# The last expert's y summed on chip through a 0/1 matrix of slots by tokens

## What is computed

```python
def grouped_moe(x, w_router, b_router, w_gate, w_up, w_down):
    gates = shared_group_router(xt, w_router, b_router)    # two experts per token
    out = jnp.zeros_like(xt)
    for e in range(N_EXPERTS):                              # 16
        h = jax.nn.silu(xt @ w_gate[e]) * (xt @ w_up[e])
        out = out + gates[:, e:e + 1] * (h @ w_down[e])
...
x = layer_norm(DN_ALPHA * x + moe, ln2_g[l], ln2_b[l])
```

## Time and profile before

| what | value |
|---|---|
| median of 3 runs | 868.54 us |
| profiled execution, its own time | 869.28 us |
| its span in the trace | 867.6 us |
| TensorE busy | 839.5 us, 97% of the span |
| VectorE, ScalarE, GpSimd busy | 566.9, 453.4, 72.4 us |
| mean granted TensorE clock | 0.98 |

### The profile page before, as it was taken

The page is one execution under the profiler, slowest core; times in us unless marked ns, Lnnn a source line. Parts: engine busy times, 40 slices in busy tenths (PEclk is TensorE's granted clock), DMA queues, the critical chain, the costliest instruction groups (busy, mean ns, idle before and its releaser), DMA issues.

```text
span 867.6 us, 11074 instructions
## 1 busy us (share of the span) xinstructions
PE 839.5 (97%) x3810; PEld 688.0 (79%) x3810; DVE 566.9 (65%) x621; ACT 453.4 (52%) x455; POOL 72.4 (8%) x61
## 2 busy tenths in 40 slices
PE   9999999999999999999999998899999999999993
PEld 8788788888888888888888887688888888888751
DVE  4887444444449874423455846699888888889607
ACT  4555434434666653323334142497878777878610
POOL 1000000000000000000000005221122111220100
PEclk9999999999999999999999978999999999999997
DMA  7242324323233333335327653899999999999552
GB/s 202 83 115 80 97 81 138 97 78 116 79 94 102 92 113 96 96 96 178 107 85 276 260 194 98 280 365 389 372 369 366 375 371 378 365 376 370 190 222 97
DMA packets 147346, 172.14 MB, mean 198 GB/s; under 512 B 7554, under 2 KB 90123, under 8 KB 147318
## 3 DMA queue, kind: packets, MB, share of 16 engines
q1 hardware_dynamic: 142214, 161.88, 55.0%
q0 software_dynamic: 5104, 9.90, 3.2%
HBM read 163.99 MB, written 15.24 MB: 207 GB/s over the span
## 4 chain that ended last, share of the span: by engine, by line
PE 63%; DMA 18%; DVE 12%; ACT 4%; issue 2%; SPq 0%; DVEq 0%; ACTq 0%; POOL 0%; POOLq 0%
DMA est<-in_w_exp_gate_dram 18%; PE psA L613 7%; PE psA L614 7%; PE psA L615 7%; DVE elo L1356 6%; PE psB L614 5%; PE psB L615 5%; PE psB L613 5%; ACT ehi L1037 3%; PE psD L613 2%; PE psD L614 2%; PE psD L615 2%; PE psC L614 1%; PE psC L615 1%; PE psC L613 1%
## 5 line engine op out<-in xcount | busy, mean ns | idle before, releaser
L1356 DVE TENSOR_TENSOR elo<-est,ehi 128x2048 fp32r<-128x2048 f32 x96 | 218.5, 2289 | 49.2 <-ACT ehi L1037 49.0
L1037 ACT ACTIVATE ehi<-est 128x2048 fp32r<-128x2048 f32 x96 | 183.1, 1917 | 72.2 <-DMA est<-in_w_exp_gate_dram 25.0
L1157 DVE TENSOR_TENSOR wlo<-wst,whi 128x1024 fp32r<-128x1024 f32 (+1 forms) x76 | 95.0, 1250 | 91.5 <-ACT whi L877 90.4
L877 ACT ACTIVATE whi<-wst 128x1024 fp32r<-128x1024 f32 (+1 forms) x76 | 81.8, 1077 | 71.6 <-PE psB L615 30.6
L784 PE MATMUL psA<-ehi,xe_hi 128*128 128x512 f32 x256 | 101.8, 398 | 2.8 <-DVE xe_lo L1553 2.8
L785 PE MATMUL psA<-elo,xe_hi 128*128 128x512 f32 x256 | 100.3, 392 | 0.0
L786 PE MATMUL psA<-ehi,xe_lo 128*128 128x512 f32 x256 | 100.2, 392 | 0.0
L613 PE MATMUL psB<-xT_hi,whi 128*128 128x512 f32 x208 | 80.9, 389 | 0.0
L614 PE MATMUL psB<-xT_lo,whi 128*128 128x512 f32 x208 | 80.9, 389 | 0.0
L615 PE MATMUL psB<-xT_hi,wlo 128*128 128x512 f32 x208 | 80.9, 389 | 0.0
L784 PEld LDWEIGHTS psA<-ehi,xe_hi 128*128 128x128 f32 x256 | 48.4, 189 | 14.4 <-DVE xe_lo L1553 2.9
(11 more groups left out here) (287 smaller groups left out, 1520.8 us busy)
## 6 DMA issues: line engine op xcount, KB each, us to landing
est<-in_w_exp_gate_dram SPq DMA_DIRECT2D x32, 1024.0 KB, 13.7
est<-in_w_exp_down_dram SPq DMA_DIRECT2D x32, 1024.0 KB, 13.9
est<-in_w_exp_up_dram SPq DMA_DIRECT2D x32, 1024.0 KB, 12.9
wst<-in_w_in_dram SPq DMA_DIRECT2D x60, 512.0 KB, 3.9
wst<-in_w_branch_r_dram SPq DMA_DIRECT2D x8, 640.0 KB, 4.4
wst<-in_w_branch_a_dram SPq DMA_DIRECT2D x8, 512.0 KB, 3.6
o_st<-in_w_out_dram SPq DMA_DIRECT2D x8, 512.0 KB, 4.6
x1d<-x SPq DMA_DIRECT2D x8, 512.0 KB, 3.9
```

The costliest lines, as they stand in the source:

```text
L877: A(whi[p][:, 0:K, :], wst[p][:, 0:K, :], ACT.Copy).then_inc(w_hi, 1)
L1037: A(ehi[s][:], est[s][:], ACT.Copy).then_inc(gu_hi if s < 4 else d_hi, 1)
L1157: V.tensor_tensor(wlo[p][:, 0:K, :], wst[p][:, 0:K, :], whi[p][:, 0:K, :], ALU.subtract).then_inc(w_lo, 1)
L1356: V.tensor_tensor(elo[s][:], est[s][:], ehi[s][:], ALU.subtract).then_inc(gu_lo if s < 4 else d_lo, 1)
```

## The change

The y of expert 15 stays on chip. ScalarE and VectorE split it, scaled, into last_hi and last_lo; VectorE builds last_by, a matrix with a 1 where a slot's token is the column's token; TensorE adds last_by times last_hi and last_lo to each tile's sum. Expert 15's scatter is dropped, so its rows of `ys` are never written; `ys` is cleared in memory by eight stores at the place where the table is cleared. SyncE's wait before it loads `ys` is now for the scatters up to expert 14 and for gate and up of expert 15. The down product of expert 14 stands between the two halves of gate and up of expert 15. x1 is added to yg by GpSimd, tile by tile, and the x1 products and the filler are dropped.

```diff
--- before.py
+++ after.py
@@ -196,6 +196,9 @@
         hT_hi = at("hT_hi", 154, [P, KF, P], F32R)
         hT_lo = at("hT_lo", 156, [P, KF, P], F32R)
         yb = [at("yb0", 158, [P, D]), at("yb1", 72, [P, D])]
+        last_hi = at("last_hi", 72, [P, D], F32R)
+        last_lo = at("last_lo", 92, [P, D], F32R)
+        last_by = at("last_by", 104, [P, S], F32R)
         ln2_gb = at("ln2_gb", 162, [P, 2, D])
         chosen_by = at("chosen_by", 151, [P, 3, TT, P], BF16)
 
@@ -308,6 +311,10 @@
         y_evac = sem("y_evac")
         y_stored = [sem(f"y_stored{p}") for p in range(2)]
         more_stored = sem("more_stored")
+        ys_zeroed = sem("ys_zeroed")
+        last_l = sem("last_l")
+        last_listed = sem("last_listed")
+        pre_done = sem("pre_done")
         sum_done = sem("sum_done")
         ln2_landed = sem("ln2_landed")
         got = [sem(f"got{t}") for t in range(TT)]
@@ -461,7 +468,8 @@
                 sp.dma_start(ln2_gb[:, n, :], v.to_broadcast([P, D])).then_inc(ln2_landed, 16)
 
             for p in range(2):
-                sp.wait_ge(y_stored[p], (NE // 2 - p) * 16)
+                sp.wait_ge(y_stored[p], (NE // 2 - 1) * 16)
+            sp.wait_ge(gu_used, 4 * NE)
             sp.wait_ge(more_stored, more * 16 + 16)
             for t in range(TT):
                 for n in range(2):
@@ -505,8 +513,11 @@
             pool.wait_ge(tile_done, 20)
             pool.dma_start(tab.rearrange("(b p) w -> b p w", p=P), vacant[0:BLOCKS]).then_inc(tab_cleared, 16)
             pool.dma_start(x1d[ROWS:ROWS + P, :], zero[:]).then_inc(trash_zeroed, 16)
+            for n in range(2 * TT):
+                pool.dma_start(ys[n * P:(n + 1) * P, :], zero[:]).then_inc(ys_zeroed, 16)
             pool.wait_ge(tab_cleared, 16)
             pool.wait_ge(trash_zeroed, 16)
+            pool.wait_ge(ys_zeroed, 16 * 2 * TT)
 
             def gather(b, idx):
                 pool.indirect_dma_start(out=xe[b % 2][:], out_offset=None, in_=x1d,
@@ -518,7 +529,7 @@
                 pool.wait_ge(y_evac, b * 2 + 2)
                 pool.indirect_dma_start(out=ys, out_offset=bass.IndirectOffsetOnAxis(ap=idx, axis=0),
                                         in_=yb[b % 2][:], in_offset=None, bounds_check=ROWS - 1,
-                                        oob_is_err=False).then_inc(y_stored[b % 2] if b < NE - 1 else more_stored, 16)
+                                        oob_is_err=False).then_inc(y_stored[b % 2] if b < NE - 2 else more_stored, 16)
 
             pool.wait_ge(x1_stored, 32 * TT)
             pool.wait_ge(pick_done, 1)
@@ -542,7 +553,7 @@
                 gather(b, lists[:, b, 0:1].bitcast(U32))
                 if b >= 4:
                     scatter(b - 4, lists[:, b - 4, 0:1].bitcast(U32))
-            for b in range(NE - 4, NE):
+            for b in range(NE - 4, NE - 1):
                 scatter(b, lists[:, b, 0:1].bitcast(U32))
             pool.wait_ge(plan_done, 2)
             more = pool.value_load(plan[0:1, 7:8], min_val=0, max_val=BLOCKS - NE)
@@ -561,6 +572,9 @@
                     pool.indirect_dma_start(out=ys, out_offset=bass.IndirectOffsetOnAxis(ap=cur[:, 0:1].bitcast(U32),
                                                                                          axis=0),
                                             in_=yb[0][:], in_offset=None).then_inc(more_stored, 16)
+            for t in range(TT):
+                pool.wait_ge(got[t], 32)
+                nc.gpsimd.tensor_tensor(yg[:, 0, t, :], yg[:, 0, t, :], x1[:, t, :], ALU.add).then_inc(pre_done, 1)
 
 
         @block.tensor
@@ -773,9 +787,9 @@
                                       xe[p][:, k * P:(k + 1) * P], ident[:])
                 mm.then_inc(xe_t, 1)
 
-            def gate_up(b, first=False):
+            def gate_up(b, first=False, parts=range(4)):
                 pe.wait_ge(xe_l, b + 1)
-                for s in range(4):
+                for s in parts:
                     if s % 2 == 0 and not first:
                         pe.wait_ge((silu_done, h_done)[s // 2], b)
                     pe.wait_ge(gu_lo, b * 4 + (s + 1))
@@ -836,13 +850,15 @@
                 turn(2 * i, 1, xe_landed[1], i * 16 + 16)
                 turn(2 * i + 1, 0, xe_landed[0], i * 16 + 32)
             turn(NE - 2, 1, xe_landed[1], NE // 2 * 16)
-            gate_up(NE - 1)
+            gate_up(NE - 1, parts=range(2))
             down(NE - 2)
+            gate_up(NE - 1, parts=range(2, 4))
             hidden_t(NE - 1)
             down(NE - 1)
             pe.wait_ge(plan_done, 2)
             more = pe.value_load(plan[0:1, 7:8], min_val=0, max_val=BLOCKS - NE)
             with pe.If(more > 0):
+                pe.wait_ge(last_l, 2)
                 with pe.Fori(0, more) as i:
                     rows_t(i + NE, 0, more_landed, i * 16 + 16)
                     gate_up(i + NE)
@@ -850,17 +866,21 @@
                     down(i + NE)
 
             for t in range(TT):
+                pe.wait_ge(pre_done, t + 1)
                 if t == TT - 1:
                     pe.wait_ge(y_evac, (more + NE) * 2)
-                    warm(18, psB[0])
+                    pe.wait_ge(last_l, 2)
                 for h in range(2):
-                    pe.matmul(pairs[t][:, h, :], ident[:], x1[:, t, h * S:(h + 1) * S], start=True, stop=False)
-            for t in range(TT):
-                pe.wait_ge(got[t], 32)
-                for n in range(2):
-                    for h in range(2):
-                        mm = pe.matmul(pairs[t][:, h, :], ident[:], yg[:, n, t, h * S:(h + 1) * S],
-                                       start=False, stop=(n == 1))
+                    for n in range(2):
+                        pe.matmul(pairs[t][:, h, :], ident[:], yg[:, n, t, h * S:(h + 1) * S],
+                                  start=(n == 0), stop=False)
+                if t == 0:
+                    pe.wait_ge(last_listed, 1)
+                    pe.wait_ge(last_l, 2)
+                for h in range(2):
+                    for part in (last_hi, last_lo):
+                        mm = pe.matmul(pairs[t][:, h, :], last_by[:, t * P:(t + 1) * P], part[:, h * S:(h + 1) * S],
+                                       start=False, stop=(part is last_lo))
                 mm.then_inc(sum_done, 1)
 
 
@@ -963,6 +983,7 @@
 
             act.wait_ge(tab_cleared, 16)
             act.wait_ge(trash_zeroed, 16)
+            act.wait_ge(ys_zeroed, 16 * 2 * TT)
             with act.Fori(0, KD // 2) as i:
                 for p in range(2):
                     act.wait_ge(tile_done, 2 * i + (N_BA + p + 1))
@@ -1118,16 +1139,16 @@
                 turn(b)
 
             silu(NE - 1)
-            e_round(NE - 1, 4)
-            y_out(NE - 2, 0)
+            for s in range(2):
+                e_round(NE - 1, 4 + s)
+                y_out(NE - 2, s)
             hidden_round(NE - 1)
-            e_round(NE - 1, 5)
-            y_out(NE - 2, 1)
+            act.wait_ge(y_stored[1], (NE // 2 - 1) * 16)
             for s in range(2):
-                y_out(NE - 1, s)
+                act.wait_ge(d_used, NE * 2 - 1 + s)
+                A(last_hi[:, s * DF:(s + 1) * DF], psB[s], ACT.Copy, scale=lists[:, NE - 1, 1:2].bitcast(F32)).then_inc(y_evac, 1)
             act.wait_ge(plan_done, 2)
             more = act.value_load(plan[0:1, 7:8], min_val=0, max_val=BLOCKS - NE)
-            act.wait_ge(y_stored[0], NE // 2 * 16)
             with act.If(more > 0):
                 with act.Fori(0, more) as i:
                     b = i + NE
@@ -1585,10 +1606,26 @@
             turn(0, prev=False, first=True)
             with dve.Fori(1, NE - 1) as b:
                 turn(b)
+            e_rest(NE - 1, 4)
+            dve.wait_ge(lists_landed, 16)
+            token, tail = keys[:, 0, :], keys[:, 1, :]
+            chain.link(V.tensor_copy(token[:, 0:1], lists[:, NE - 1, 0:1]))
+            chain.link(V.tensor_scalar(token[:, 1:2], token[:, 0:1], float(S), -float(S), ALU.is_ge, ALU.mult))
+            chain.link(V.tensor_tensor(token[:, 0:1], token[:, 0:1], token[:, 1:2], ALU.add))
+            for t in range(TT):
+                ins = V.tensor_scalar(tail[:, t:t + 1], token[:, 0:1], -float(t * P), None, ALU.add)
+            chain.link(ins)
+            for t in range(TT):
+                ins = V.tensor_scalar(last_by[:, t * P:(t + 1) * P], slots[:], tail[:, t:t + 1], None, ALU.is_equal)
+            ins.then_inc(last_listed, 1)
+            e_rest(NE - 1, 5)
             hidden(NE - 1)
-            e_rest(NE - 1, 4)
             hidden_rest(NE - 1)
-            e_rest(NE - 1, 5)
+            for s in range(2):
+                dve.wait_ge(y_evac, NE * 2 - 1 + s)
+                half = slice(s * DF, (s + 1) * DF)
+                V.scalar_tensor_tensor(last_lo[:, half], psB[s], lists[:, NE - 1, 1:2].bitcast(F32),
+                                       last_hi[:, half], ALU.mult, ALU.subtract).then_inc(last_l, 1)
             dve.wait_ge(plan_done, 2)
```

## The result

The changed kernel takes 873.01 us (median of 7 runs, 871.16 to 874.1). The kernel before, run beside it, takes 868.81. The ratio is 1.005, with an interval of 1.0035 to 1.0065: **slower by 0.5%, some 4.3 us**, where 865.3 was predicted. Its span is 1.9 us longer than the one before, while the medians differ by 4.2.

What follows compares the result with a forecast made beforehand. The end was taken as set by when tile 1's sum is done on TensorE, VectorE's rounds following. Move +6.0, work removed after the product -9.2, clearing 0: -3.2 us, from the 868.54 median to 865.3, range 863.4 to 868.8.

Steps and rivals of the forecast that it cites:

- Cost 0, at most 1.5 us: Early stage, from about 142 us: eight clearing stores drain by about 154, so the weight load lands in time.
- the slow stretch that I charged to each pause of the tail: Eight matmuls at 1.2 GHz, 1.6 us, after each new TensorE pause of 4.2 and 2.8 us.
- lands 4.1 us later: Tail: expert 14's scatter starts at 823.0 and lands at 827.1, so y loads start at 827.2, 6.5 us earlier.
- Each before TensorE wants it: Tail: GpSimd's x1 adds ready at 834.6, 837.3, 839.9, 842.6; TensorE wants them at 835.1, 839.4, 843.8, 848.1.
- The move's cost: Tail: moving expert 14's down product makes expert 15's end at 835.1, 6.0 us later than 829.03.
- The adds of 2.3 us: Tail: each GpSimd x1 add of one tile takes 2.3 us, estimated from a 128x128 cast.
- the four short matmuls: Tail, per tile: four matmuls of the 0/1 matrix, 0.227 us each, add 0.91 us.
- -9.2: After expert 15's down product: x1 products and filler gone, 17.9 us to tile 1's statistics becomes 8.7, 9.2 less.
- The pauses eat it: Rival, 0.31: the tail's new pauses hold the clock low longer, 4.8 us instead of 1.6; time 866.0 to 868.5.
- The clearing delays the early stage: Rival, 0.06: clearing ys takes 1.5 us off the gain; time 867.0.
- GpSimd becomes the bound: Rival, 0.08 with slower than before: tail adds of 5.0 us or more lose; 5.9 each gives 872.3.
- the wait for y outlasts the down product: Sign of a wrong forecast: in the tail, the wait for y lasts longer than expert 15's down product.

Runs made afterwards that it cites:

- e3: Kernel before with only expert 14's down product moved between the halves of expert 15's gate and up, ScalarE and VectorE orders to suit: 874.05 us, ratio 1.0066.
- e5: e2 with VectorE's list work moved ahead of both split rests of expert 15's down weights: 865.79 us, ratio 0.9962 to the kernel before.
- e1: Kernel before with only the eight clearing stores of ys added, in one burst: 871.31 us, ratio 1.0039.
- e2: The changed kernel with its eight clearing stores spread, one per weight tile: 868.55 us, ratio 1.0001 to the kernel before.
- e4: e2 with expert 14's down product put back behind all of expert 15's gate and up, list work ahead of est4's rest: 867.93 us, ratio 1.0003.
- e9: e4 with both halves of expert 14's y written in a row and tile 0's x1 added on TensorE: 860.99 us, ratio 0.9914 to the kernel before.
- e8: The changed kernel with its clearing, still one burst, cut into 512-byte pieces: 874.13 us, ratio 1.0068 to the kernel before.
- e7: e4 with 16 filler matmuls on TensorE ahead of the wait for the first add: 866.29 us, ratio 0.9976 to the kernel before.
- e10: e9 with all four x1 adds on GpSimd: 863.36 us, ratio 0.9953 to the kernel before.
- e6: e4 with x1 of tiles 0 and 1 as products on TensorE, tiles 2 and 3 on GpSimd: 863.92 us, ratio 0.9959 to the kernel before.

## Why the prediction was wrong

The sum was 6.0 - 9.2 + 0 = -3.2. The runs give +5.7 for the move (e3), -9.0 for what comes off behind it when the trip is in time (e5 against e3), 3.4 to 4.3 for the clearing (e1, and e2 against the change), and 3.4 for a term that wasn't there (e5 against e2). That makes 5.7 - 9.0 + 3.4 to 4.3 + 3.4 = +3.5 to +4.4, against a measured +4.3. The three terms of the tail meet in e2 by the way they are taken, so they test nothing; the test is the clearing, measured by e1 and again by what e2 gains on the change, and the two differ by 0.9 us, less than their intervals are wide.

The traces give a second reading of the tail, free of what happens before it. Us from the start of expert 15's gate and up to the end of its down product, and from there to tile 1's statistics (from these to the end of the span it is 20.65 to 20.74 in every trace):

| trace | to the end of the product | from there to tile 1's statistics | sum |
|---|---|---|---|
| before | 26.24 | 17.90 | 44.14 |
| forecast | 32.3 | 8.7 | 41.0 |
| the change | 31.36 | 12.63 | 43.99 |
| e3 move only | 32.26 | 18.06 | 50.32 |
| e5 list work first | 31.36 | 9.84 | 41.20 |
| e4 no move | 26.28 | 17.38 | 43.66 |
| e9 y of 14 sooner | 24.94 | 12.06 | 37.00 |

The tail of the change is thus neutral by itself, and its loss lies before expert 15. Behind the product it went over the forecast by 3.9 us in the change and by 1.1 in e5.

**Clearing ys: "Cost 0, at most 1.5 us": the first step that failed.** The deadline was right: TensorE ran dry at 155.8, forecast 156.4. The landing was not. I divided all bytes by the rate and let the load be done at 154; it landed at 156.6. The rate of 396 GB/s from the tail was too high (352 from 141 to 157 us), the 512 KB of zeros for x1d, issued just ahead, were left out, and the load got its last bytes at the burst's end. So the bound should have been a stall of 2 to 3 us. And the slow stretch that I charged to each pause of the tail, 1.6 us, I didn't charge to this one, though the window at 159.9 shows it just the same. What e1 and e2 show is 3.4 to 4.3.

The Trainium skill (DMA: Bandwidth & Descriptors, section Queues, rings and completion order) says that a DMA engine takes turns between its queues packet by packet, a packet being some 9 to 17 descriptors. From 141 to 175 us e1 has 1328 packets of 4.74 MB on GpSimd's queue, 3.6 KB each, and 5200 of 2.62 MB on SyncE's, 0.5 KB each. Whether the profile counts the page's packets or single descriptors, no run shows. If the turns go one for one by the profile's count, a load of some 1040 small packets gets through beside as many large ones, of the 1152 that eight stores are (1328 less the 176 of the kernel before), and so near the end of the burst. The landings fit that: the load landed at 156.6, and the last two stores, issued after 145 us, took 11.1 us to land in the mean, which is until about 156.5. But that is argued, not shown; the run made to test it, e8, didn't.

**Expert 14's scatter "lands 4.1 us later": the second.** This was the landing of a scatter that begins 1.3 us after its neighbouring elo. In my own times the list work put the last elo at 823.1 to 825.4 and the scatter at 823.0: side by side from the start. I used the two scatters, 1.82 and 0.97 us, only to price a rival about the adds, and not for the scatter itself. In the trace it ends 0.86 us after the elo, as in rows 3 and 5 (827.56 and 828.42 here, 824.59 and 825.44 before). It lands 5.24 us after its start. The Trainium skill (SBUF — State Buffer, section SBUF: two separate sides) has a lock that fits: VectorE with two inputs in SBUF, once it has started, keeps an instruction of GpSimd that reads SBUF out until it has finished; e5, where only the order changes, agrees (the scatter takes 1.83 us and ends 0.86 us after the elo).

**"Each before TensorE wants it": the third, which follows from the second for the most part.** The first add was to be ready 0.5 us before the down product ended, a margin below every error around it. It came 1.9 us too late, and even with the scatter on time (e5) 0.83 us too late. And a wait there costs more than its length: the sum behind it took 5.40 instead of 3.43, at a clock of 0.65. I charged slow stretches to the two pauses that I knew, and none to a third that I had ruled out. What the change removes is also what covered this: before, 11 us of x1 products and filler stood between the down product and the first y. e4 shows the wait that is left without that cover and with the product in its old place (6.11 us), e7 that filler alone brings back 2.4 us.

**Where it was right.** The move's cost (6.0, measured 5.7) and the pauses in it: those of 4.2 and 2.8 us came as 4.16 and, with the transposes between, 0.84 + 0.66 + 1.41 = 2.91. What the clock adds was right only in sum, and by luck. After the second pause I charged 1.6 us, but the down product of 15 ran 24 matmuls in 5.75 us at full clock, and TensorE was done at 836.2 where 835.1 plus the 2.0 lost early makes 837.1. After the first pause I charged 1.6 too, and in e3 the product took 8.3 us instead of 5.45, 2.9 more: the two errors nearly cancel there. The adds of 2.3 us took 2.34 to 2.41, the four short matmuls 0.93 against 0.91. And -9.2 was -9.0 by the ratios once the trip was in time; by the traces of the table, -8.1.

**The rivals.** None was the case. "The pauses eat it" named the wrong pause, though e3 shows that the first can hold the clock down for 13 matmuls. "The clearing delays the early stage" had the right mechanism and less than half of its price. "GpSimd becomes the bound" had the lock right and the instruction wrong: not the adds, which met no elo, but the scatter ahead of them. I had written that the forecast fails if the wait for y outlasts the down product; it did.

**What stays open.** How two queues share a DMA engine in detail (e8), and why the clock stays high after one pause and not after another of the same length (below); each kernel has one kept trace, so how often each happens isn't known.

## What to carry to other kernels

Work taken off an engine is worth only what remains when the next thing that it covered comes to light: list, for each removed filler or product, the transfer behind it, and compare arrival and need with a margin that is larger than the errors of both. A "free" burst on an idle queue is to be priced against the next small load on another queue, as if that load ended with the burst; here spreading it brought back the 4.3 us (e2). A scatter issued by GpSimd is to be placed beside VectorE's two-input passes on paper before it is costed; a few short instructions moved ahead of such a pass were worth 3.4 us here.

## What the runs showed of the hardware

- One 512 KB load beside a burst of eight 512 KB stores on another queue took 14.0 us to land, beside four 9.3, in the kernel before 4.0.
- A scatter beside an elo ended 0.85 to 0.87 us after it, wherever it began: it took 3.01 us when both started together, 1.83 when the elo started 1.3 us sooner (e5), 0.98 when the elo was ending (e9), as beside nothing. It landed after 5.24, 4.04 and 3.21 us.
- The low clock doesn't follow from a pause's length alone. The same pause of 1.83 us ahead of the same product was followed by 0.51 before and by 1.00 in e7. After single waits of 1.91 (the change), 3.83 (e10) and 6.11 us (e4) the sum of tile 0 took 5.40, 5.33 and 5.96 us; after 0.83 (e5), 1.55 (e6) and 1.81 (e7, behind filler) it took 3.70, as did the sum of tile 1 after 1.15 (e9). The two pauses of 0.84 and 1.41 us with transposes between them were followed by 24 matmuls at full clock.
